# Gate/up products of an FFN as seven block products in place of eight, with the hidden tiles through DRAM

## The chip, the cores and the metric

One core of one Trainium2 chip runs the kernel. The metric is the device time in microseconds (us), a median of several executions. TensorE (PE in the profile) multiplies, VectorE (DVE) and ScalarE (ACT) work on tiles, GpSimd is POOL, and SyncE (SP) issues nearly all DMAs.

## The reference

Two blocks follow each other: a two-layer mixer (not touched here), then a hybrid layer of three attention-like mixers whose end is a gated FFN. Tokens T = 1024, model width D = 1024, hidden width 2816. All in fp32:

```python
x = layer_norm(ALPHA * x + mix @ w_out, ln1_g, ln1_b)
gu = jnp.einsum('bsd,df->bsf', x, w_gu)
gate, up = gu[..., :FFN_HIDDEN], gu[..., FFN_HIDDEN:]
ffn = jnp.einsum('bsf,fd->bsd', jax.nn.silu(gate) * up, w_down)
return layer_norm(DEEPNORM_ALPHA * x + ffn, ln2_g, ln2_b)
```

## The kernel before

Activations lie transposed: width on the 128 partitions (KT = 8 tiles k of width), tokens along the row, in two halves of 512. An fp32 product is made as three fp32r products: each operand is split in a high part (rounded) and a low part (what is left), and `w_hi*x_hi + w_lo*x_hi + w_hi*x_lo` are summed in PSUM. x1, the FFN's input, is split in `act_hi` and `act_lo`.

Weights come in **units**. SP loads a block of 128 columns (8 x 128 rows) into `w_raw[u % 2]` once the unit two before has been split. ACT rounds it into `w_hi[u % 2]` as soon as PE is done with the unit two before (`hi_at` L779, in loops `hi_next` L786), DVE makes `w_lo` (L1341, L1347), and PE multiplies. `product` (L2157) takes a unit over both halves of the tokens: 8 k x 3 x 2 = 48 matmuls of 128x512, each weight block for two of them in turn. `half_product` (L2176) takes a unit over one half, 24 matmuls; `half_pair` (L2192) does two units with their k interleaved.

The hidden width has FB = 22 tiles f of 128 columns, in GROUPS of 4, 6, 6, 6. A tile needs a gate unit and an up unit. f = 0 and 1 (SPLIT) are done by halves, while the layer norm of the second half of x1 is still under way (`x1_lo` L1858, `ln_center` L1834). For each other f, PE runs two `product`s into PSUM pairs 0 and 1, ACT takes silu of the gate (L1162), DVE multiplies by the up tile into `f_buf` (L1915), ACT rounds into `f_hi` (L1166) and DVE makes `f_lo` (L1919). After each group but the last come 8 down units, one for each output tile d (`down_rows`, L2622, PSUM pairs 2 and 3), and DVE adds each into the accumulator `z` (L1937). `z` starts as ALPHA * (x1 + bias), made by `x1_start` (L1864) in half tiles between the layer norm's steps. The last group's down products run by half for the first 512 tokens (L2192, L2176, unit U_LAST on) with transposes of z between them (L2664), and then the other way round, tokens on the partitions, for the rest (L2694), followed by the output's layer norm. In the FFN's start, PE's variance sums of the second half (L2576) wait for four `x1_start`s; the late squares are added at L1899.

PE's order of work in the FFN:

```python
for g, n in enumerate(GROUPS):
    with loop(pe, n - first) as j:
        for r, pair_used in ((0, g_act), (1, f_mul)):
            product(ug + 2 * (j + first) + r, (ug + r) % 2, r)
    if g < len(GROUPS) - 1:
        with loop(pe, KT // 2) as j:
            ...
```

Of the kernel before, what the change touches and what calls it, by code (L numbers as in the profile page):

```python
# [10 lines left out]
ALU = mybir.AluOpType  # L11
# [49 lines left out]

FG = 6
# [82 lines left out]

class Tally:
# [34 lines left out]
def build(nc, x, c, w_ada, b_ada, g_pre, w_in, w_conv, w_pool, pool_scale, w_out, g_post,  # L181
# [8 lines left out]
    x_mid = nc.dram_tensor("x_mid", [P, KT, T], FP32).ap()  # L190
    w_ada_v = w_ada.rearrange("l (p t) n -> l p t n", t=KT)

    with ExitStack() as ctx:
# [95 lines left out]
        with over() as t:  # L289
            t("under_tail", [P, 3 * KT + 1, T])  # L290
            tail = t("tail", [P, 3, T])
        arena = sb("arena", [P, ARENA])
# [16 lines left out]
        sub_gain = sb("sub_gain", [P, 1])  # L309
        index_w = sb("index_w", [P, TT, IH])  # L310
# [87 lines left out]
        U_GROUP = [U_FFN + sum(2 * n + KT for n in GROUPS[:g]) + (SPLIT if g else 0) for g in range(len(GROUPS))]  # L398
        U_LAST = U_GROUP[-1] + 2 * GROUPS[-1]
        U_END = U_LAST + 2 * KT  # L400
# [24 lines left out]

        bits_done, cand_ready, signs_done = sem("bits_done"), sem("cand_ready"), sem("signs_done")
# [46 lines left out]
        def out_stat(t, c_):  # L473

            return o_ss[:, t, c_:c_ + 1]

# [20 lines left out]
        def _(sp):  # L497
# [88 lines left out]
            def load_down(u, slot, g, d):  # L586
                n = GROUPS[g]
                sp.wait_ge(hi_ready, 1 + u)
                sp.wait_ge(lo_ready, 1 + u)
                sp.dma_start(w_raw[slot][:, 0:n, :], w_down_v[:, F_AT[g]:F_AT[g] + n, bass.ds(d * P, P)])\  # L590
                  .then_inc(raw_loaded[slot], 16)

            for g, n in enumerate(GROUPS):
                ug = U_GROUP[g]
                first = 0
                if g == 0:
                    for q in range(2 * SPLIT):
                        load(ug + q, (ug + q) % 2, w_gu(q % SPLIT // 2, q % 2))
                    ug, first = ug + SPLIT, SPLIT // 2
                with loop(sp, n - first) as j:  # L600
                    for r in range(2):
                        load(ug + 2 * (j + first) + r, (ug + r) % 2, w_gu(F_AT[g] + j + first, r))
                if g < len(GROUPS) - 1:
                    with loop(sp, KT // 2) as j:
                        for r in range(2):
                            load_down(ug + 2 * n + 2 * j + r, (ug + r) % 2, g, 2 * j + r)
            for q in range(KT):
                load_down(U_LAST + q, (U_LAST + q) % 2, len(GROUPS) - 1, q)
                if q == 1:
                    sp.dma_start(g_row[:], ln2_g.broadcast_to([P, D])).then_inc(rows_loaded, 16)  # L610
# [133 lines left out]
        def _(act):  # L744
# [419 lines left out]
            def f_rounded(f, at):  # L1164
                act.wait_ge(f_mul, 1 + f + 1)
                A(f_hi[:, bass.ds(at, 1), :], f_buf[:].rearrange("p (a t) -> p a t", a=1), ACT.Copy)\  # L1166
                    .then_inc(f_hi_done, 1)

            for f in range(SPLIT // 2):
                hi_at(U_FFN + SPLIT + 2 * f + 2)  # L1170
                gated(f, 2 * f)
                hi_at(U_FFN + SPLIT + 2 * f + 3)
                f_rounded(f, f)

            for g, n in enumerate(GROUPS):
                last = g == len(GROUPS) - 1
                ug, first = U_GROUP[g], 0
                if g == 0:
                    ug, first = ug + SPLIT, SPLIT // 2
                act.wait_ge(unit_done, 1 + ug + 2 * first + 1)  # L1180
                with loop(act, n - first) as j:
                    f = F_AT[g] + first + j
                    hi_next(ug + 2 * first, j, 2, 0)
                    gated(f, 0)
                    hi_next(ug + 2 * first, j, 2, 1)
                    f_rounded(f, first + j)
                if not last:
                    with loop(act, KT // 2) as j:
                        for r in range(2):
                            hi_next(ug + 2 * n, j, 2, r)  # L1190
# [11 lines left out]
            for d in range(KT):  # L1202
                if d + 2 < KT:
                    hi_at(U_LAST + d + 2)
# [37 lines left out]
        def _(dve):  # L1242
# [649 lines left out]

            lo_at(U_FFN + 2)
            ln_center(1, range(KT))
            x1_start(0, range(3))
# [4 lines left out]
            x1_start(0, range(3, KT))  # L1900
# [10 lines left out]
            dve.sem_inc(acc_added, 2)  # L1911

            def f_product(f, f_bank):
                dve.wait_ge(g_act, 1 + f + 1)
                v.tensor_tensor(f_buf[:], silu_buf[:], bank[f_bank + 1][:], ALU.mult).then_inc(f_mul, 1)  # L1915

            def f_low(f, at):
                dve.wait_ge(f_hi_done, f + 1)
                v.tensor_tensor(f_lo[:, bass.ds(at, 1), :].rearrange("p a t -> p (a t)"), f_buf[:],  # L1919
                                f32(f_hi[:, bass.ds(at, 1), :].rearrange("p a t -> p (a t)")), ALU.subtract)\  # L1920
                    .then_inc(f_lo_done, 1)
                dve.wait_ge(f_lo_done, f + 1)

            for f in range(SPLIT // 2):
                lo_at(U_FFN + SPLIT + 2 * f + 2)
                if f == 0:
                    x1_start(1, range(KT))
                    dve.wait_ge(acc_init, 2 * KT)
                lo_at(U_FFN + SPLIT + 2 * f + 3)
                dve.wait_ge(unit_done, 2 + U_FFN + SPLIT + 2 * f + 2)  # L1930
                f_product(f, 2 * f)
                f_low(f, f)

            def accumulate(d, b, a=None):
                zz = z[:, bass.ds(d, 1), :].rearrange("p a t -> p (a t)") if a is None else z[:, d, half(a)]
# [3 lines left out]
            for g, n in enumerate(GROUPS):  # L1939
                last = g == len(GROUPS) - 1  # L1940
                ug, first = U_GROUP[g], 0
                if g == 0:
                    ug, first = ug + SPLIT, SPLIT // 2
                dve.wait_ge(unit_done, 1 + ug + 2 * first + 1)
                with loop(dve, n - first) as j:
                    f = F_AT[g] + first + j
                    lo_next(ug + 2 * first, j, 2, 0)
                    lo_next(ug + 2 * first, j, 2, 1)
                    f_product(f, 0)
                    f_low(f, first + j)  # L1950
                if not last:
                    with loop(dve, KT // 2) as j:
                        for r in range(2):
                            dve.wait_ge(unit_done, 3 + ug + 2 * n + 2 * j + r)
                            accumulate(2 * j + r, 2 + r)
                            lo_next(ug + 2 * n, j, 2, r)
                    dve.wait_ge(acc_added, 2 + (g + 1) * KT)
# [10 lines left out]
            for d in range(KT):  # L1968
                if d + 2 < KT:
                    lo_at(U_LAST + d + 2)  # L1970
# [72 lines left out]
        def _(pe):  # L2043
# [692 lines left out]
```

## Time and profile before

| | us |
|---|---|
| median of 3 runs (lowest, highest) | 2164.23 (2163.54, 2164.96) |
| span of the profiled execution | 2160.5 |
| PE busy | 2110.7 |
| DVE busy | 1088.7 |
| ACT busy | 748.4 |
| POOL busy | 177.8 |

The span runs from the first to the last instruction of one execution; of that execution the profile gives no other time, so the runs' median stands 3.7 us above it. Engines work side by side, and their busy times overlap. DMA moved 154.75 MB, 72 GB/s in the mean.

### The profile page before, as it was taken

What the parts mean: (1) busy time and instruction counts of PE and PEld (TensorE: products, weight loads), DVE (VectorE), ACT (ScalarE), POOL (GpSimd) and SP (SyncE); (2) the same over time, 40 slices, a digit from 0 to 9 for tenths busy, and PEclk for the clock granted to TensorE, in tenths of its full rate; (3) what the DMA queues carried; (4) which work ended last, traced back from release to release, by engine and by line L of the source; (5) the groups of instructions that cost most, each with busy time, mean ns of one, the idle gap of its engine ahead of it and who ended that gap; (6) DMA issues with size and microseconds to landing.
All of it is one profiled execution on the core that took longest, in us unless ns stands there. A gap on an engine that the chain in (4) does not pass through costs nothing.

```text
span 2160.5 us, 25819 instructions
## 1 busy us (share of the span) xinstructions
PE 2110.7 (98%) x9846; PEld 1682.4 (78%) x9846; DVE 1088.7 (50%) x1701; ACT 748.4 (35%) x1191; POOL 177.8 (8%) x159
## 2 busy tenths in 40 slices
PE   8999999999999999999989998999999999999998
PEld 4888888888888877688866667778888888888877
DVE  6834463663334373888877784572422222232246
ACT  4311124431112444665766663342111111111133
POOL 1000002300000231011200000310000000000000
PEclk9999999999999999999989999999999999999999
DMA  8532333222111423101100003321211121112131
GB/s 305 166 117 88 98 106 95 76 73 69 41 47 49 134 85 88 50 22 30 49 20 1 1 21 117 90 68 53 64 49 44 44 59 49 39 49 59 46 129 78
DMA packets 222092, 154.75 MB, mean 72 GB/s; under 512 B 6565, under 2 KB 209462, under 8 KB 221878
## 3 DMA queue, kind: packets, MB, share of 16 engines
q1 hardware_dynamic: 215392, 134.53, 20.5%
q0 software_dynamic: 4608, 16.78, 2.4%
q10 hardware_dynamic: 2006, 2.31, 0.3%
q8 instruction: 53, 0.87, 0.2%
q14 instruction: 33, 0.27, 0.0%
HBM read 145.21 MB, written 8.39 MB: 71 GB/s over the span
## 4 chain that ended last, share of the span: by engine, by line
PE 84%; DVE 7%; ACT 5%; issue 2%; POOL 1%; SPq 1%; DMA 1%; DVEq 0%; ACTq 0%; POOLq 0%
PE pair L2157 37%; PE pair L2176 17%; PE pair L2622 8%; PE pair L2369 4%; PE pair L2222 3%; PE pair L2505 3%; PE pair L2473 2%; ACT proj L1007 2%; PE pair L2402 2%; PE pair L2694 2%; PE pair L2487 1%; DVE act_region L1721 1%; PE pair L2390 1%; PE pair L2192 1%; DVE w_lo L1341 1%
## 5 line engine op out<-in xcount | busy, mean ns | idle before, releaser
L1347 DVE TENSOR_TENSOR w_lo<-w_raw,w_hi 128x1024 fp32r<-128x1024 f32 x101 | 123.6, 1223 | 560.2 <-ACT w_hi L786 560.0
L786 ACT ACTIVATE w_hi<-w_raw 128x1024 fp32r<-128x1024 f32 x102 | 108.3, 1061 | 797.9 <-PE pair L2157 621.0
L2157 PE MATMUL pair<-act_hi,w_hi 128*128 128x512 f32 x1168 | 361.2, 390 | 0.0
L2157 PE MATMUL pair<-act_hi,w_lo 128*128 128x512 f32 x1168 | 359.6, 389 | 0.0
L2157 PE MATMUL pair<-act_lo,w_hi 128*128 128x512 f32 x1168 | 359.6, 389 | 0.0
L2157 PEld LDWEIGHTS pair<-act_hi,w_hi 128*128 128x128 f32 x1168 | 218.9, 188 | 46.8 <-issue 1.0
L2157 PEld LDWEIGHTS pair<-act_lo,w_hi 128*128 128x128 f32 x1168 | 219.2, 188 | 45.6
L2157 PEld LDWEIGHTS pair<-act_hi,w_lo 128*128 128x128 f32 x1168 | 219.2, 188 | 45.6
L2176 PE MATMUL pair<-act_hi,w_hi 128*128 128x512 f32 x608 | 244.4, 402 | 2.8 <-ACT act_hi L796 1.2
L2176 PE MATMUL pair<-act_lo,w_hi 128*128 128x512 f32 x608 | 238.7, 393 | 0.0
L2176 PE MATMUL pair<-act_hi,w_lo 128*128 128x512 f32 x608 | 238.2, 392 | 0.0
L1341 DVE TENSOR_TENSOR w_lo<-w_raw,w_hi 128x1024 fp32r<-128x1024 f32 x88 | 111.4, 1266 | 175.0 <-ACT w_hi L779 168.1
L779 ACT ACTIVATE w_hi<-w_raw 128x1024 fp32r<-128x1024 f32 x86 | 91.1, 1059 | 225.8 <-PE pair L2176 208.4
L2176 PEld LDWEIGHTS pair<-act_hi,w_hi 128*128 128x128 f32 x608 | 115.1, 189 | 29.9 <-issue 5.0
L2176 PEld LDWEIGHTS pair<-act_hi,w_lo 128*128 128x128 f32 x608 | 115.2, 190 | 25.6 <-issue 2.4
L2176 PEld LDWEIGHTS pair<-act_lo,w_hi 128*128 128x128 f32 x608 | 114.9, 189 | 25.1 <-DVE act_lo L1858 0.3
L2505 PEld LDWEIGHTS pair<-v_all,act_region 128*128 128x128 f32 x576 | 71.2, 196 | 32.3 <-issue 16.9
L1937 DVE TENSOR_TENSOR z<-pair,z 128x1024 f32 (+1 forms) x32 | 34.9, 1090 | 110.3 <-PE pair L2622 107.1
L2505 PE MATMUL pair<-v_all,act_region 128*128 128x128 f32 (+1 forms) x576 | 80.1, 286 | 2.0 <-ACT act_region L1071 2.0
L2622 PE MATMUL pair<-f_hi,w_hi 128*128 128x512 f32 x256 | 79.1, 390 | 0.0
L2622 PE MATMUL pair<-f_lo,w_hi 128*128 128x512 f32 x256 | 78.9, 389 | 0.0
L2622 PE MATMUL pair<-f_hi,w_lo 128*128 128x512 f32 x256 | 78.8, 389 | 0.0
(416 smaller groups left out, 3177.4 us busy)
## 6 DMA issues: line engine op xcount, KB each, us to landing
w_raw<-w_in SPq DMA_DIRECT2D x76, 512.0 KB, 3.8
w_raw<-w_out SPq DMA_DIRECT2D x48, 512.0 KB, 3.8
w_raw<-w_gu SPq DMA_DIRECT2D x48, 512.0 KB, 3.8
w_raw<-w_down SPq DMA_DIRECT2D x24, 384.0 KB, 3.2
act_region<-w_ada SPq DMA_DIRECT2D x16, 512.0 KB, 13.8
sq<-w_ada POOLq DMA_DIRECT2D x16, 512.0 KB, 4.5
sq_sum<-w_ada POOLq DMA_DIRECT2D x16, 512.0 KB, 4.9
yT<-x SPq DMA_DIRECT2D x8, 512.0 KB, 7.2
```

The source lines that it names most:

```text
L779: A(w_hi[u % 2][:], w_raw[u % 2][:], ACT.Copy).then_inc(hi_ready, 1)
L786: A(w_hi[s_][:], w_raw[s_][:], ACT.Copy).then_inc(hi_ready, 1)
L1007: A(sign_out[i], score[:, sel_at(i):sel_at(i) + keys(i)], ACT.Sign, bias=f32(cand[:, q:q + 1]), accum_out=cnt[:, q:q + 1]).then_inc(signs_ ...
L1341: v.tensor_tensor(w_lo[u % 2][:], w_raw[u % 2][:], f32(w_hi[u % 2][:]), ALU.subtract)\
L1347: v.tensor_tensor(w_lo[s_][:], w_raw[s_][:], f32(w_hi[s_][:]), ALU.subtract)\
L2157: i = mm(bank[pair][:, h * HALF:(h + 1) * HALF], w[slot][:, k, :], a[:, k, h * HALF:(h + 1) * HALF], start=(k == 0 and w is w_hi and a is ...
L2176: i_ = mm(o, w[u % 2][:, k, :], x_[:, k, tokens], start=(k == order[0] and w is w_hi and x_ is hi), stop=(k == order[-1] and x_ is lo))
L2222: i = mm(bank[pair][:, half(h)], w[slot][:, k, :], a[:, k, half(h)], start=(k == 0 and w is w_hi and a is act_hi), stop=(k == KT - 1 and w ...
L2369: i_ = mm(o, x_[:, k, t * P:(t + 1) * P], w[:, k, :], start=(k == 0 and c_ == 0), stop=(k == KT - 1 and c_ == 2))
L2402: i_ = mm(bank[pair][:, h * HALF:(h + 1) * HALF], w[u % 2][:, k, :], a[:, k, h * HALF:(h + 1) * HALF], start=(k == 0 and w is w_hi and a i ...
L2505: i_ = mm(o, probT[g % 2][:, t * P:(t + 1) * P], w, start=(t == 0), stop=(t == i))
L2622: i_ = mm(bank[2 + r][:, half(h)], w[slot][:, k, :], x_[:, k, half(h)], start=(k == 0 and w is w_hi and x_ is f_hi), stop=(k == n - 1 and ...
```

## The change

For the 20 tiles f = 2 to 21 (PAIRS), the gate and the up columns of a tile and the two halves of x1's width and of its tokens are taken as a 2x2 block product: blocks of x1 of 4 k-tiles x 512 tokens, blocks of weights of 4 k-tiles x 128 columns. The eight block products are replaced by seven (Strassen's scheme in Winograd's form): four of them need sums of x1's blocks (T1 to T4, made once by DVE and split by ACT and DVE) and four need sums of weight blocks (`weight_sums`, for each pair). A block product is `gu_product`, 12 matmuls of 128x512. Some add into a PSUM bank that holds an earlier one, others are added by DVE (`u2`, `gate1_sum`, `up_sums`), and ACT copies two out (`p1_keep`, `p5_keep`). The four halves of PSUM used by a pair alternate between pairs.

All pairs run first, then the down units of the first three groups (`down_product`), then the last group as before. The products f go from `f_buf` to DRAM (`f_mid`) and are loaded again into `f_raw` when the down units need them, to be split then. `f_raw` and `w_sum` are the same memory. All loops of the FFN are written out. `x1_start` works on whole tiles, one in each of pairs 1 to 8, in place of half tiles in the layer norm; ACT rounds and DVE splits down weights only over a group's tiles (n x 128 columns in place of 1024).

The diff, cut to its core:

```diff
+KB = KT // 2
+PAIRS = FB - SPLIT // 2
+MS = 7
...
+        M_ACT = [(x1_block(act_hi, 0, 0), x1_block(act_lo, 0, 0)), (T_HI[T4], T_LO[T4]),
+                 (x1_block(act_hi, KB, 0), x1_block(act_lo, KB, 0)), (T_HI[T1], T_LO[T1]), (T_HI[T2], T_LO[T2]),
+                 (x1_block(act_hi, KB, 1), x1_block(act_lo, KB, 1)), (T_HI[T3], T_LO[T3])]
+        M_BANK = (0, 3, 0, 1, 2, 1, 2)
+        M_MORE = (2, 5, 6)
...
+            load_pair(0)
+            keep_f(0)
+            load_pair(1)
+            keep_f(1)
+            load_pair(2)
+            for p in range(3, PAIRS):
+                keep_f(SPLIT // 2 + p - 3)
+                load_pair(p)
...
+            def m_round(p, i):
+                if p:
+                    act.wait_ge(*m_done.at(MS * (p - 1) + i + 1))
...
+                A(m_weight(True, i), m_source(i), ACT.Copy).then_inc(m_hi.sem, 1)
...
+                    down_round(0)
+                    f_round(0)
+                    f_round(1)
+                    down_round(1)
...
-            x1_start(0, range(3))
             lo_at(U_FFN + 3)
...
-            x1_start(0, range(3, KT))
+            dve.sem_inc(late_summed, 1)
             ln_root(1)
...
+                v.tensor_tensor(w_sum[:, 0], u0, u1, ALU.add).then_inc(w_summed.sem, 1)
+                dve.wait_ge(*w_summed.at(4 * p + 1))
+                v.tensor_tensor(w_sum[:, 1], w_sum[:, 0], g0, ALU.subtract).then_inc(w_summed.sem, 1)
+                dve.wait_ge(*w_summed.at(4 * p + 2))
+                v.tensor_tensor(w_sum[:, 2], g1, w_sum[:, 1], ALU.subtract).then_inc(w_summed.sem, 1)
+                v.tensor_tensor(w_sum[:, 3], g0, u0, ALU.subtract).then_inc(w_summed.sem, 1)
...
+            t_sums()
+            lo_at(U_FFN + SPLIT + 2)
+            t4_sums()
+            dve.wait_ge(unit_done, 2 + U_FFN + SPLIT + 2)
+            f_product(0, 0)
+            lo_at(U_FFN + SPLIT + 3)
+            for i, n in enumerate((T4, T1)):
+                for a in range(2):
+                    t_low(n, a)
+                m_low(0, i)
+            weight_sums(0)
...
+            for p in range(PAIRS):
+                more = p < PAIRS - 1
+                if p:
+                    m_low(p, MS - 1)
+                    up_sums(p - 1)
+                    pair_product(p - 1)
+                if p == 0:
+                    u2(p)
+                if more:
+                    weight_sums(p + 1)
+                    for i in range(4):
+                        m_low(p + 1, i)
...
+                if p:
+                    u2(p)
+                if more:
+                    m_low(p + 1, 4)
...
+                gate1_sum(p)
+                if more:
+                    m_low(p + 1, 5)
+                if 1 <= p <= KT:
+                    x1_start(p - 1)
+            up_sums(PAIRS - 1)
+            pair_product(PAIRS - 1)
...
+            for a in range(N_DOWN):
+                g, d = divmod(a, KT)
+                down_low(a + 2)
+                dve.wait_ge(unit_done, 2 + U_DOWN + a + 1)
+                if g:
+                    dve.wait_ge(acc_added, 2 + a - KT + 1)
+                accumulate(d, a % 2)
+                if d < GROUPS[g + 1]:
+                    f_low(F_AT[g + 1] + d)
...
+            def gu_product(p, i):
+
+                pe.wait_ge(*m_hi.at(MS * p + i + 1))
+                pe.wait_ge(*m_lo.at(MS * p + i + 1))
...
+                if i == 2:
+                    pe.wait_ge(*p1_kept.at(p + 1))
+                if i == 5:
+                    pe.wait_ge(*p5_kept.at(p + 1))
+                if i == 6:
+                    pe.wait_ge(*u2_made.at(p + 1))
...
+                for k in range(KB):
+                    if p == 0 and M_T[i] is not None:
+                        pe.wait_ge(*t_lo.at(2 * M_T[i] + k // 2 + 1))
+                    for w, x_ in ((hi, x_hi), (lo, x_hi), (hi, x_lo)):
+                        i_ = mm(o, w[:, k, :], x_[:, k, :], start=(k == 0 and w is hi and x_ is x_hi and i not in M_MORE),
+                                stop=(k == KB - 1 and x_ is x_lo), skip_group_check=i in M_MORE)
+                i_.then_inc(m_done.sem, 1)
...
+            for p in range(PAIRS):
+                for i in range(MS):
+                    gu_product(p, i)
+            pe.sem_inc(unit_done, 2 * PAIRS)
+            for a in range(N_DOWN):
+                down_product(a)
```

## Rows read from the trace of the kernel before

**Rows 1.** The page: span, PE's busy time, PE's granted clock in 40 slices
```profile
span 2160.5 us, 25819 instructions
...
PE 2110.7 (98%) x9846; PEld 1682.4 (78%) x9846; DVE 1088.7 (50%) x1701; ACT 748.4 (35%) x1191; POOL 177.8 (8%) x159
...
PEclk9999999999999999999989999999999999999999
```

**Rows 2.** The chain of waits over the FFN: start us, us, what
```profile
1555.27 130.74 PE pair L2157 x576
...
1686.01 65.28 PE pair L2622 x288
...
1947.13 130.57 PE pair L2157 x576
```

**Rows 3.** Windows, one gate/up stretch: us, busy by engine, PE clock, DMA share, GB/s
```profile
1555.00:1686.00 131.00, 131.00 (x579) 108.36 (x578) 27.68 (x24) 23.52 (x23) 0.00 (x0) 1.00 0.17 49
```

**Rows 4.** Timeline of the last down group's start, idle before in brackets
```profile
2077.53 0.39 PE L2192 MATMUL pair<-f_hi,w_hi 128*128 128x512 f32 x1
...
2080.20 0.19 PEld L2192 LDWEIGHTS pair<-f_hi,w_hi 128*128 128x128 f32 x1 [0.89 <-issue]
...
2083.88 0.19 PEld L2192 LDWEIGHTS pair<-f_lo,w_hi 128*128 128x128 f32 x1 [0.64 <-DVE f_lo L1919]
...
2087.46 0.19 PEld L2176 LDWEIGHTS pair<-f_hi,w_hi 128*128 128x128 f32 x1 [0.74 <-DVE z L1937]
```

**Rows 5.** Timeline of PE: first matmul of two half products, first behind them
```profile
1456.68 0.42 PE L2176 MATMUL pair<-act_hi,w_hi 128*128 128x512 f32 x1
...
1467.61 0.62 PE L2157 MATMUL pair<-act_hi,w_hi 128*128 128x512 f32 x2
```

**Rows 6.** Groups by shape, 1590 to 2160 us: busy us, mean ns | idle before
```profile
L1347 DVE TENSOR_TENSOR w_lo<-w_raw,w_hi 128x1024 fp32r<-128x1024 f32 x50 | 61.1, 1223 | 272.6 <-ACT w_hi L786 272.6
...
L786 ACT ACTIVATE w_hi<-w_raw 128x1024 fp32r<-128x1024 f32 x49 | 52.0, 1062 | 364.8 <-PE pair L2157 258.4 <-PE pair L2622 106.4
...
L1937 DVE TENSOR_TENSOR z<-pair,z 128x512 f32<-128x512 f32 x8 | 5.5, 685 | 3.2 <-PE pair L2176 3.2
```

**Rows 7.** The same view from 1380 to 1460 us, two half-tile operations
```profile
L1119 ACT ACTIVATE sq<-z 128x512 f32<-128x512 f32 x4 | 2.5, 633 | 4.8 <-DVE z L1834 3.9 <-POOL sum L734 0.9
...
L1899 DVE TENSOR_TENSOR f_buf<-f_buf,rstd_diag 128x512 f32<-128x512 f32 x1 | 0.7, 693 | 0.0
```

**Rows 8.** Timelines of DVE and PE in the FFN's start
```profile
1423.91 3.35 DVE L1864 TENSOR_SCALAR z<-z,params 128x512 f32<-128x512 f32 x3
...
1429.10 0.39 PE L2176 MATMUL pair<-act_lo,w_hi 128*128 128x512 f32 x1
...
1430.39 1.02 PE L2576 MATMUL pair<-ones,sum 128*128 128x1 f32 x8 [0.90 <-DVE z L1864]
...
1449.69 1.63 DVE L1858 SCALAR_TENSOR_TENSOR act_lo<-z,params,act_hi 128x512 fp32r<-128x512 f32 x2
...
1455.26 1.23 DVE L1341 TENSOR_TENSOR w_lo<-w_raw,w_hi 128x1024 fp32r<-128x1024 f32 x1 [3.94 <-ACT w_hi L779]
...
1456.40 3.25 DVE L1864 TENSOR_SCALAR z<-z,params 128x512 f32<-128x512 f32 x8
```

**Rows 9.** DMA issues, 1500 to 2160 us: count, KB each, us to landing
```profile
w_raw<-w_gu SPq DMA_DIRECT2D x36, 512.0 KB, 3.8
...
out<-tail SPq DMA_DIRECT2D x3, 512.0 KB, 2.6
```

**Rows 10.** Windows, columns as in rows 3, at half and at full clock
```profile
1433.40:1436.40 3.00, 3.00 (x9) 2.32 (x8) 0.28 (x1) 0.51 (x1) 0.00 (x0) 0.50 0.00 0
...
1440.30:1446.00 5.70, 3.14 (x11) 1.55 (x11) 5.28 (x8) 3.00 (x4) 0.00 (x0) 1.00 0.31 92
...
1447.00:1450.30 3.30, 3.30 (x10) 2.61 (x9) 3.30 (x6) 1.94 (x3) 0.00 (x0) 0.51 0.54 157
...
2078.00:2088.00 10.00, 8.94 (x37) 6.51 (x36) 5.41 (x5) 5.29 (x6) 0.00 (x0) 1.00 0.71 250
```

More of the change, by code:

```diff
@@ L397, in build @@
         U_FFN = U_OUT2 + 2 * KT
-        U_GROUP = [U_FFN + sum(2 * n + KT for n in GROUPS[:g]) + (SPLIT if g else 0) for g in range(len(GROUPS))]
-        U_LAST = U_GROUP[-1] + 2 * GROUPS[-1]
-        U_END = U_LAST + 2 * KT
+        U_GU = U_FFN + 2 * SPLIT
+        U_DOWN = U_GU + 2 * PAIRS
+        N_DOWN = (len(GROUPS) - 1) * KT
+        U_LAST = U_DOWN + N_DOWN
         ROW2_LN = [0, 2 * KT]
@@ L1175, in _, with t_round @@
[L1175 to L1190, printed above, removed]
+            def t_round(n, a):
+                act.wait_ge(*t_sum.at(((8, 10), (1, 2), (4, 6), (12, 14))[n][a]))
+                A(T_HI[n][:, 2 * a:2 * a + 2, :], T_RAW[n][:, 2 * a:2 * a + 2, :], ACT.Copy).then_inc(t_hi.sem, 1)
@@ new lines, in p1_keep, with p5_keep @@
+            def p1_keep(p):
+                act.wait_ge(*m_done.at(MS * p + 1))
+                if p >= 2:
+                    act.wait_ge(*up0_made.at(p - 1))
+                    act.wait_ge(*up1_made.at(p - 1))
+                A(p1_buf(p), quarter(p, 0), ACT.Copy).then_inc(p1_kept.sem, 1)
+            def p5_keep(p):
+                act.wait_ge(*m_done.at(MS * p + 4))
+                if p:
+                    act.wait_ge(*up1_made.at(p))
+                A(junk[:], quarter(p, 1), ACT.Copy).then_inc(p5_kept.sem, 1)
@@ new lines, in m_low, with u2 @@
+            def m_low(p, i):
+                dve.wait_ge(*m_hi.at(MS * p + i + 1))
+                v.tensor_tensor(m_weight(False, i), m_source(i), f32(m_weight(True, i)), ALU.subtract).then_inc(m_lo.sem, 1)
+            def u2(p):
+                dve.wait_ge(*m_done.at(MS * p + 5))
+                dve.wait_ge(*p1_kept.at(p + 1))
+                dve.wait_ge(f_mul, 1 + SPLIT // 2 + p)
+                v.tensor_tensor(silu_buf[:, half(1)], quarter(p, 2), p1_buf(p), ALU.add).then_inc(u2_made.sem, 1)
@@ new lines, in pair_product, with x1_start @@
+            def pair_product(p):
+                dve.wait_ge(*gate0_act.at(p + 1))
+                dve.wait_ge(*gate1_act.at(p + 1))
+                dve.wait_ge(*up0_made.at(p + 1))
+                dve.wait_ge(*up1_made.at(p + 1))
+                v.tensor_tensor(f_buf[:], silu_buf[:], f_buf[:], ALU.mult).then_inc(f_mul, 1)
+            def x1_start(k):
+                dve.wait_ge(*t_sum.at(14))
+                v.tensor_scalar(z[:, k, :], z[:, k, :], ln_b(k), ALPHA, ALU.add, ALU.mult).then_inc(acc_init, 1)
@@ L1934, in accumulate @@
             def accumulate(d, b, a=None):
-                zz = z[:, bass.ds(d, 1), :].rearrange("p a t -> p (a t)") if a is None else z[:, d, half(a)]
+                zz = z[:, d, :] if a is None else z[:, d, half(a)]
                 o = bank[b][:] if a is None else bank[b][:, half(a)]
                 v.tensor_tensor(zz, o, zz, ALU.add).then_inc(acc_added, 1)
[L1939 to L1957, printed above, removed]
@@ L2656, in f_split @@
+            for p in range(PAIRS):
+                for i in range(MS):
+                    gu_product(p, i)
+            pe.sem_inc(unit_done, 2 * PAIRS)
+            for a in range(N_DOWN):
+                down_product(a)
             def f_split(k, low):
```

413 lines of the change are left out of this document (321 added, 92 removed).

## The prediction

> **What bounds the kernel now.** I read the page first: TensorE (PE) is busy 98% of 2160.5 us at a granted clock of 9 tenths or more in nearly every slice [rows 1]. A busy PE may still be slow, so the second view is the chain of waits over the FFN. From 1511 to 2077 us it is nothing but matmuls: stretches of 576 of gate/up products (L2157) and of 288 of down products (L2622) in turn, each of which begins where the last ended [rows 2]. 130.74 us by 576 gives **0.227 us a matmul** of 512 columns, and 65.28 by 288 the same 0.2267: no gap at a unit's border, nor at a turn of the loops. So every matmul taken out of the FFN is worth 0.2267 us, as long as the other engines stay ahead. The third view is who does what in an FFN stretch: in 131 us with six tiles VectorE (DVE) is busy 27.7 us and ScalarE (ACT) 23.5 [rows 3]. There is much room behind PE.
>
> From 2077.7, where the third stretch of 576 ends, to 2087.5 the chain is not on PE, which looks like a stall of 9.8 us. It is not: PE ran 36 matmuls in it, worth 8.16. The timeline shows three holes: PE's weight loads waited 0.89 us (the second down weight split too late), 0.64 (last `f_lo`) and 0.74 (accumulator added late) [rows 4]. From 2077.53 to 2087.49 is 9.96 us, so 1.8 us are lost.
>
> **Matmuls removed.** Before, one hidden tile f costs 2 units x 8 k x 3 x 2 halves = 96 matmuls. After, `gu_product` makes 7 products x 4 k x 3 = 84. 20 tiles (PAIRS) take part; f = 0 and 1 stay half products. 20 x 12 = 240 matmuls x 0.2267 = **-54.4 us**. A weight now serves one matmul where in `product` it served two. The half products are already like that: 48 of them, over two units, start at 1456.68 and end their turn at 1467.61, 0.2277 each [rows 5]. Hence the weight load costs nothing visible, since one of 0.19 us [rows 4] lies beside a matmul's 0.227. The excess of 0.05 us is at the first boundary, whose weights came 0.19 us before [rows 8]; at the second one there is none. For the 140 borders between products I take 0, since the operands should be ready 2 us or more before; the other bound is 0.05 x 140 = 7 us. A gain at a border is excluded, as 0.2267 is already the pitch.
>
> **The 24 down units** of three groups keep their matmuls; they move behind the pairs: cost 0, if their operands are there (below).
>
> **DVE and ACT per pair.** A pair takes PE 84 x 0.2267 = 19.04 us (before 21.76). Half tiles of 512 cost DVE 0.68 to 0.69 from PSUM or SBUF, and whole ones 1.22; ACT 0.63 and 1.06 [rows 6, 7]. DVE does 7 `m_low`, 4 weight sums and 5 sums of products, 16 x 0.68 = 10.9, the product 1.2, and in eight pairs `x1_start`, 0.8 (before, 8 half tiles took 3.25 us [rows 8], so two take 0.8): 12.9 us. ACT: 7 roundings, 2 copies, 2 silus, 11 x 0.63 = 6.9. Both lie under 19.04. What decides is order. I put times from the start of pair p on PE, whose products end each 2.72. DVE: m_low(p,6) until 1.4, `up_sums(p-1)` and `pair_product(p-1)` until 4.8, weight sums of p+1 until 7.6, low parts 0 to 2 until 10.0. ACT waits for product 3 (10.9), copies it (11.5), rounds weight 3 (12.1); DVE low part 12.8, waits for product 4 (13.6), `u2` 14.3. PE wants `u2` for product 6 at 16.3: slack 2.0. `p1_keep` is at 3.3 for product 2 at 5.4 (slack 2.1), `p5_keep` at 11.5 for product 5 at 13.6 (2.1). Weights of p+1 are ready a product's length or more ahead, for ACT rounds each once PE has let go of its predecessor 16 us before. Behind DVE's wait for product 4 stand weight 4's low part and `gate1_sum`; their users come 13 us and 3 products later. So steady state costs **0**, with three covers of 2 us each; if one is gone, its overrun is paid in each of 19 pairs.
>
> **SP's queue and DRAM.** SP now waits for a finished product (4.8 us into the next pair) before the store, and the next weight load stands behind it. That load also waits for low part 2 at 10.0, so the store adds no wait; two loads land 3.8 us after issue [rows 9], near 18, and are wanted by ACT at 19.0 + 2.7. No store of an FFN tile is in the trace; output stores of the same 512 KB land in 2.6 us, loads in 3.8 [rows 9]. Store and reload, 22 times each, have pairs or units of time to spare, except f = 0 to 3: f_raw lies over w_sum and so they load from 1.4 us into the last pair, two by two; I get low part 3 at 16.7, before PE's 19.04. Cost 0; the bound is one load late, 3.8 us. SP's weight loads for the down units are then ahead by a unit. In a down unit (5.4 or 8.2 us) DVE does a low part, an accumulation and an f low part, at most 3.7 us, ACT 2.1: covered. f = 21 is ready 3.4 us into the down phase, and is wanted in the last group.
>
> **The start.** x1_start of the first half leaves the chain before the second half's variance. There DVE took 3.35 us for three pieces, and then those of the second call; PE had begun its half product's last matmul at 1429.10 and at a pitch of 0.227 was free at 1429.33, but its next began at 1430.39 [rows 8]. Without it PE does not wait: **-1.1 us**. After the last `x1_lo` (1451.3) DVE now has T1 and T2 first: 2 x 1.15 + 4 x 0.69 = 5.1 us, then w_lo of the next half product: 1457.6 where it was 1456.5, and PE wanted it at 1456.68 [rows 5, 8]: **+1.1 us**. Then T4 sums, product of f = 0, w_lo (1462.6), two T4 low parts, low part of weight 0 (1465.6), T1, low part 1 (1468.5), four sums (1471.2), two T2 low parts, low part 2 (1474.2); in this order `gu_product(0,0)` starts at 1468.6, product 2 could at 1474.0 and starts at 1474.2. ACT has four more of 1.06 in between and the loads of GATE and UP at 1461 and 1466; I take **+0.5** for the whole of it, bounds 0 and 3. Products 3 to 6 have T3 and `u2` ready at 1484.1 and 1484.8 for 1485.9.
>
> **The tail.** f's are ready long before; U_LAST+1's weights take 0.8 + 0.9 (768 columns) after the last down unit, under the nine matmuls (2.04 us) that `half_pair` does before it asks for them; ACT has no f to wait for. **-1.8 us**, bounds -1.8 and 0.
>
> Sum: -54.4 - 1.8 - 1.1 + 1.1 + 0.5 = **-55.7**; span 2160.5 - 55.7 = 2104.8. The runs' median is 2164.2, 3.7 above the span of the profiled execution, so **2108.5**.
>
> **The clock.** Twice in the FFN's start it is at half (1.2 GHz): 3.0 us after a 1 us pause and light matmuls of one column, 3.3 us after a stretch in which PE was idle 2.6 of 5.7 us [rows 10]. Nine and ten matmuls stood where 14 would: 1.5 us each. I leave both in place. In the tail, with three holes under 0.9 us in 10, it stayed whole [rows 10]. So small holes at borders should not lower it. The Trainium skill says otherwise in "TensorE: Matmul & The Clock Gate", section "A second HAM failure mode: psum-queue depth-cycling": a kernel that cycled through PSUM banks at each iteration paused briefly so often that its clock kept falling. The change halves the matmuls between two banks. By that rule the time would be that of rival B, 2175, and by the rows that of the sum.
>
> **Rivals.**
> A. *Borders cost.* 140 x 0.05 = 7 us: 2115.5. For: the one late border. Against: 576 matmuls without a gap. 12%.
> B. *One cover missed in each pair and the clock falls.* Place: PE at product 6 for `u2`, or 5 for `p5_keep`. A hole of 1.3 us or more, with half clock for 3 us behind it (1.5 us), makes 2.8 us a pair, and 20 x 2.8 = 56 is the point from which it decides. With a hole of 2 us: 3.5 x 19 = 66, 2108.5 + 66 = 2175, slower than before. For: a chain of six semaphores between engines per pair where there was one. Against: DVE would have to be 3.3 us later than worked out. 4%.
> C. *A cover missed by half a us*, without the clock: 19 x 0.5 = 9.5: 2118. 10%.
> D. *The low clock stretches go*, as the 1 us pause goes: -1.5 to -4.5: 2104 to 2107. For: the pause ahead of the first one goes. Against: the light matmuls and DVE's late `x1_lo` stay. 15%.
> E. *The start has a hole of 3 us more than taken*, T tiles queueing on DVE: 2111.5. 15%.
> Forecast as worked out: 44%.
>
> **Range.** A, C and E reach 2118, D 2104; unknown loads add 3.8 to one of them. 2103 to 2119 leaves out B and the far ends. Faster by over 0.2% (4.3 us, what a measurement of this kernel can tell): all but B and a larger mishap, 0.95; within 0.2% 0.01; slower 0.04.
>
> **What would show it.** PE: 1680 matmuls of `gu_product` at a pitch of 0.227 and a pair each 19.04 us; no idle of PE on `silu_buf`, `rstd_diag` or `junk`; chain all PE between the pairs and down products; DVE some 13 us of each 19. Wrong if the pitch is above 0.229 (A), if PE waits for DVE once a pair (B, C), if the clock in the pairs is under 1.00 (B), or if the handover to the down products has a hole over 1 us.

## The result and the profile after

| | before | after |
|---|---|---|
| median of 4 runs, us (lowest, highest) | 2164.24 (2163.54, 2164.96) | 2106.36 (2105.71, 2107.17) |
| ratio to before, 95% interval | | 0.9735 [0.9721, 0.9748] |
| span of the profiled execution, us | 2160.5 | 2103.6 |

The change takes 57.9 us off, 2.65%. The forecast was a median of 2108.5 and a span of 2104.8.

The page, as in [rows 1], with two rows of its DMA part:

```profile
span 2103.6 us, 25382 instructions
...
PE 2054.2 (98%) x9606; PEld 1636.5 (78%) x9606; DVE 1254.7 (60%) x1996; ACT 814.9 (39%) x1359; POOL 177.5 (8%) x159
...
PEclk9999999999999999999998999999999999999999
...
f_mid<-f_buf SPq DMA_DIRECT2D x22, 512.0 KB, 2.6
f_raw<-f_mid SPq DMA_DIRECT2D x22, 512.0 KB, 3.7
```

PE has 240 matmuls fewer (9846 to 9606) and is busy 56.5 us less, in the same share of a shorter span. DVE has 166 us more to do and ACT 66.5, and neither is seen in the time.

The chain of waits over the FFN, as in [rows 2] (L2995 is `gu_product`, L3018 `down_product`, L2542 `half_pair`, L2526 `half_product`):

```profile
1472.58 375.62 PE pair L2995 x1656
1848.20 174.08 PE pair L3018 x768
2022.28 8.36 PE pair L2542 x36
2030.64 4.33 PE pair L2526 x18
```

From 1472.58 to the tail there is nothing but matmuls, at 375.62/1656 = 0.2268 and 174.08/768 = 0.2267 us each. The handover to the down units has no hole. A stretch of this view ends with the end of its last matmul, 0.16 us after the next one has started: the timeline has the first matmul of the last group's `half_pair` at 2022.12. By the timeline this stretch takes 2030.62 - 2022.12 = 8.50 us, where it took 9.96 before [rows 4]:

```profile
2022.12 0.39 PE L2542 MATMUL pair<-f_hi,w_hi 128*128 128x512 f32 x1
...
2030.62 0.47 PE L2526 MATMUL pair<-f_hi,w_hi 128*128 128x512 f32 x1
```

All that PE itself waited for from 1380 us on (engine, line, waited for: us in total, times, longest):

```profile
PE pair L2542 <- DVE w_lo L1569: 1.8, 1, 1.8
PE pair L2526 <- DVE w_lo L1569: 0.8, 1, 0.8
PE pair L2542 <- DVE act_lo L2086: 0.7, 2, 0.4
PE pair L2526 <- DVE z L2056: 0.6, 1, 0.6
PE pair L2995 <- ACT w_hi L1321: 0.5, 1, 0.5
```

The second row and the last are the two waits that the change brings: w_lo behind T1 and T2 (L2141, L2145), and product 2 of the first pair. The view puts the last down to ACT, but product 2 also needs its own low part, which DVE finished at 1471.80 + 0.68 = 1472.48, 0.1 us before the matmul. Their places:

```profile
1455.49 0.47 PE L2526 MATMUL pair<-act_hi,w_hi 128*128 128x512 f32 x1 [0.80 <-DVE w_lo L1569]
...
1466.49 0.39 PE L2995 MATMUL pair<-act_hi,early_hi 128*128 128x512 f32 x1
...
1472.58 0.47 PE L2995 MATMUL pair<-act_hi,early_hi 128*128 128x512 f32 x1 [0.49 <-ACT w_hi L1321]
```
```profile
1471.80 0.68 DVE L2193 TENSOR_TENSOR early_lo<-w_raw,early_hi 128x512 fp32r<-128x512 f32 x1
```

DVE and ACT in the pairs, columns as in [rows 3]:

```profile
1474.00:1848.00 374.00, 374.00 (x1651) 309.68 (x1651) 241.22 (x348) 132.78 (x220) 0.00 (x0) 1.00 0.29 90
```

The 374 us hold 374/19.04 = 19.6 pairs, so DVE works 12.3 us a pair and ACT 6.8 (forecast 6.9), with the clock at 1.00. For DVE the forecast had 12.9 in the eight pairs with `x1_start` and 12.1 in the others, 12.4 in the mean. And the cover of `u2` (L2199), in one pair whose first product starts at 1638.60; product 6 starts at 1654.92, 16.3 us in:

```profile
1638.60 0.39 PE L2995 MATMUL pair<-act_hi,early_hi 128*128 128x512 f32 x1
...
1654.92 0.39 PE L2995 MATMUL pair<-act_hi,w_hi 128*128 128x512 f32 x1
```
```profile
1650.83 0.69 DVE L2193 TENSOR_TENSOR w_lo<-w_sum,w_hi 128x512 fp32r<-128x512 f32 x1 [2.03 <-ACT w_hi L1321]
1652.40 0.69 DVE L2199 TENSOR_TENSOR silu_buf<-pair,rstd_diag 128x512 f32<-128x512 f32 x1 [0.88 <-PE pair L2995]
```

`u2` ends at 1653.09, 14.5 us in; the forecast had 14.3 and a slack of 2.0, the trace 1.8. ACT's two copies in the same pair:

```profile
1641.52 0.60 ACT L1328 ACTIVATE rstd_diag<-pair 128x512 f32<-128x512 f32 x1 [2.09 <-PE pair L2995]
...
1649.68 0.60 ACT L1334 ACTIVATE junk<-pair 128x512 f32<-128x512 f32 x1 [1.60 <-PE pair L2995]
```

`p1_keep` ends at 1642.12 and product 2 starts at 1644.04, `p5_keep` ends at 1650.28 and product 5 starts at 1652.20: 1.9 us of slack each (forecast 2.1). `u2` is the tightest cover, by 0.1 us.

**Which stretches to compare.** The same first row of the FFN's start lies anywhere from 1384.88 us (e6) to 1391.70 (e10) in the traces, though nothing ahead of it was changed. So I compare two stretches of the traces. *Start*: from the variance sums of the first half (first PE row of L2576, L2926 after) to the first full gate/up matmul. *Middle*: from there to the first half product of the tail (for the kernels with all pairs ahead, where that is said, to the first down product). The rows that give the start, for before, after, e3, e4, e8 and e10 in this order, one fence a kernel:

```profile
1386.57 1.05 PE L2576 MATMUL pair<-ones,sum 128*128 128x1 f32 x8
```
```profile
1387.08 1.05 PE L2926 MATMUL pair<-ones,sum 128*128 128x1 f32 x8
```
```profile
1391.04 1.05 PE L2576 MATMUL pair<-ones,sum 128*128 128x1 f32 x8
...
1470.45 0.62 PE L2157 MATMUL pair<-act_hi,w_hi 128*128 128x512 f32 x2
```
```profile
1388.16 1.05 PE L2577 MATMUL pair<-ones,sum 128*128 128x1 f32 x8
...
1466.41 0.61 PE L2158 MATMUL pair<-act_hi,w_hi 128*128 128x512 f32 x2
```
```profile
1389.72 1.05 PE L2932 MATMUL pair<-ones,sum 128*128 128x1 f32 x8
...
1468.24 0.39 PE L3001 MATMUL pair<-act_hi,early_hi 128*128 128x512 f32 x1
```
```profile
1391.70 0.49 PE L2932 MATMUL pair<-ones,sum 128*128 128x1 f32 x3
...
1468.07 0.39 PE L3001 MATMUL pair<-act_hi,early_hi 128*128 128x512 f32 x1
```

| start, us | before | after | e3 | e4 | e8 | e10 |
|---|---|---|---|---|---|---|
| length | 81.04 | 79.41 | 79.41 | 78.25 | 78.52 | 76.37 |

Before, 1467.61 [rows 5] - 1386.57 = 81.04; after 1466.49 - 1387.08 = 79.41. The other traces of the changed kernel whose start was left as it is (e1, e2, e5, e6, e7, e9) have 79.37 to 79.42. The middle is 2087.49 - 1467.61 = 619.88 before and 2030.62 - 1466.49 = 564.13 after: -55.75. With -1.63 in the start and +0.51 ahead of it, that is the 56.9 us of the spans.

### The profile page after: what moved, and what is told of

It is laid out like the page before. It is cut to its first block, busy times and chain, and to the rows that moved or that the text cites. A ratio compares the mean times of both kernels' runs of the same rounds, so it can differ in the third digit from the quotient of the medians.

```text
span 2103.6 us, 25382 instructions
## 1 busy us (share of the span) xinstructions
PE 2054.2 (98%) x9606; PEld 1636.5 (78%) x9606; DVE 1254.7 (60%) x1996; ACT 814.9 (39%) x1359; POOL 177.5 (8%) x159
## 4 chain that ended last, share of the span: by engine, by line
PE 84%; DVE 6%; ACT 5%; issue 2%; SPq 1%; POOL 1%; DMA 1%; DVEq 0%; ACTq 0%; POOLq 0%
PE pair L2526 19%; PE pair L2995 18%; PE pair L2507 17%; PE pair L3018 8%; PE pair L2719 4%; PE pair L2572 3%; PE pair L2855 3%; PE pair L2823 2%; ACT proj L1149 2%; PE pair L2752 2%; PE pair L3066 2%; PE pair L2837 1%; DVE act_region L1949 1%; PE pair L2740 1%; PE pair L2542 1%
## 5 line engine op out<-in xcount | busy, mean ns | idle before, releaser
L2526 PE MATMUL pair<-act_hi,w_hi 128*128 128x512 f32 x608 | 243.8, 401 | 3.4 <-DVE w_lo L1569 1.6
L2526 PE MATMUL pair<-act_lo,w_hi 128*128 128x512 f32 x608 | 238.0, 391 | 0.0
L2526 PE MATMUL pair<-act_hi,w_lo 128*128 128x512 f32 x608 | 237.7, 391 | 0.0
L1569 DVE TENSOR_TENSOR w_lo<-w_raw,w_hi 128x1024 fp32r<-128x1024 f32 x80 | 102.6, 1283 | 159.2 <-ACT w_hi L921 152.2
L1575 DVE TENSOR_TENSOR w_lo<-w_raw,w_hi 128x1024 fp32r<-128x1024 f32 x37 | 45.3, 1226 | 236.7 <-ACT w_hi L928 236.5
L928 ACT ACTIVATE w_hi<-w_raw 128x1024 fp32r<-128x1024 f32 x38 | 40.3, 1061 | 345.7 <-PE pair L2507 307.0
L921 ACT ACTIVATE w_hi<-w_raw 128x1024 fp32r<-128x1024 f32 x78 | 82.6, 1059 | 211.1 <-PE pair L2526 196.0
L2507 PE MATMUL pair<-act_hi,w_hi 128*128 128x512 f32 x528 | 164.1, 392 | 0.0
L2507 PE MATMUL pair<-act_hi,w_lo 128*128 128x512 f32 x528 | 162.6, 389 | 0.0
L2507 PE MATMUL pair<-act_lo,w_hi 128*128 128x512 f32 x528 | 162.5, 389 | 0.0
L2526 PEld LDWEIGHTS pair<-act_hi,w_hi 128*128 128x128 f32 x608 | 114.8, 189 | 30.5 <-issue 5.5
L2526 PEld LDWEIGHTS pair<-act_hi,w_lo 128*128 128x128 f32 x608 | 114.8, 189 | 25.5 <-issue 2.4
L2526 PEld LDWEIGHTS pair<-act_lo,w_hi 128*128 128x128 f32 x608 | 114.6, 189 | 24.9 <-DVE act_lo L2086 0.3
L2507 PEld LDWEIGHTS pair<-act_hi,w_hi 128*128 128x128 f32 x528 | 98.9, 188 | 21.6 <-issue 0.7
L2507 PEld LDWEIGHTS pair<-act_hi,w_lo 128*128 128x128 f32 x528 | 99.1, 188 | 20.7
L2507 PEld LDWEIGHTS pair<-act_lo,w_hi 128*128 128x128 f32 x528 | 99.1, 188 | 20.7
L2193 DVE TENSOR_TENSOR w_lo<-w_sum,w_hi 128x512 fp32r<-128x512 f32 x80 | 55.1, 692 | 67.1 <-ACT w_hi L1321 67.1
L1321 ACT ACTIVATE w_hi<-w_sum 128x512 fp32r<-128x512 f32 x80 | 50.1, 629 | 92.7 <-PE pair L2995 90.9
```

The lines of the kernel that those rows point to most:

```text
L921: A(w_hi[u % 2][:], w_raw[u % 2][:], ACT.Copy).then_inc(hi_ready, 1)
L1321: A(m_weight(True, i), m_source(i), ACT.Copy).then_inc(m_hi.sem, 1)
L1569: v.tensor_tensor(w_lo[u % 2][:], w_raw[u % 2][:], f32(w_hi[u % 2][:]), ALU.subtract)\
L1575: v.tensor_tensor(w_lo[s_][:], w_raw[s_][:], f32(w_hi[s_][:]), ALU.subtract)\
L2193: v.tensor_tensor(m_weight(False, i), m_source(i), f32(m_weight(True, i)), ALU.subtract).then_inc(m_lo.sem, 1)
L2507: i = mm(bank[pair][:, h * HALF:(h + 1) * HALF], w[slot][:, k, :], a[:, k, h * HALF:(h + 1) * HALF], start=(k == 0 and w is w_hi and a is ...
```

## The experiments

Each ran beside the kernel before on the same chip (medians 2163.5, 2163.6 and 2162.5 in the three groups e1 to e4, e5 to e8, e9 and e10).

**e1. Eight products again.** In `gu_product`:

```diff
+                if i == 0:
+                    for k in range(KB):
+                        for w, x_ in ((hi, x_hi), (lo, x_hi), (hi, x_lo)):
+                            mm(o, w[:, k, :], x_[:, k, :], start=(k == 0 and w is hi and x_ is x_hi),
+                               stop=(k == KB - 1 and x_ is x_lo))
                 for k in range(KB):
```

> The changed kernel with product 0 of each pair made twice into the same PSUM bank, so eight products a pair again: 20 x 12 = 240 matmuls more, same result. My theory (the gain is the number of matmuls, at 0.2267 us each, and all else comes to -3.5 us: tail, start, clock): 2106.4 + 54.4 = 2160.8 us, no hole of PE in the pairs. Rival (part of the gain is from the new order of the work, the written-out loops or the down units in one stretch): then adding the matmuls back costs the same 54.4, but the eight-product kernel would have to stand well below the kernel before by more than the 3.5 us that the trace accounts for. Second rival (PE had free time in the pairs): less than 54.4, such as 40.

Measured: 2160.91, ratio to before 0.9985 [0.9976, 0.9995]. Two rows of its chain of waits (L2994 is the added product):

```profile
1491.75 19.04 PE pair L3000 x84
1510.79 2.72 PE pair L2994 x12
```

Each pair is 19.04 + 2.72 = 21.76 us, what two units took before. So the eighth product is the whole gain but for 2.6 us (2163.49 - 2160.91; by the interval 1.1 to 5.2). The trace accounts for 2.0 of them outside the pairs: 1.5 in the tail and 0.5 in the first group's down units (43.98 us for 192 matmuls before, which at 0.2267 are 43.5). What the new order, the loops and DRAM bring or cost besides lies within that interval.

**e2. Fewer still.** Product 3 over one k-tile:

```diff
-                for k in range(KB):
+                ks = 1 if i == 3 else KB
+                for k in range(ks):
...
-                                stop=(k == KB - 1 and x_ is x_lo), skip_group_check=i in M_MORE)
+                                stop=(k == ks - 1 and x_ is x_lo), skip_group_check=i in M_MORE)
```

> The changed kernel with product 3 of each pair over one k-tile in place of four (it leaves out three quarters of that block product): 20 x 9 = 180 matmuls fewer. My theory (PE is still the bound at seven products, with the chains of DVE and ACT 3 us ahead): -40.8 us, 2065.6, or some us more where the copy of product 3 and u2 come late, since the pair is only 17.0 us and DVE has 13 us of work in it. Rival (DVE or the chain of semaphores is the next bound close behind): less than 30 us gained and PE holes before product 5 or 6.

Measured: 2067.91, 38.5 less than the changed kernel. The gate/up stretch, from its first matmul at 1468.87 to the first down product at 1810.11 (by the chain of waits, here and below), is 341.2 us where it is 1848.20 - 1466.49 = 381.7 in the changed kernel: -40.5 of the -40.8. The 2.0 us that the runs show less lie outside it: the work ahead of the FFN ends 2.4 us later in e2's trace (variance sums at 1389.46 us, 1387.08 in the changed kernel's). PE waited 0.4 us in the stretch in all, for the copy of product 3 (`junk`), in the first pair. PE is still the only bound at 17.0 us a pair, so the covers of the other engines hold for a further tenth.

**e3. The kernel before with the FFN's loops written out.** `with loop(pe, n - first) as j:` becomes `for j in range(n - first):`, and so for the other engines and the down units.

> The kernel before with the FFN's loops written out, nothing else. My theory: 2164.2, no difference, as the trace of before shows no gap at a turn of the loops (576 matmuls in 130.57 us). Rival (written-out loops are a part of the gain): 1 to 3 us less.

Measured: 2161.87, ratio 0.9994 [0.9984, 1.0003]: no difference. The middle is 619.6 us (2090.07 - 1470.45) beside 619.9.

This run taught something by the way. Its start is 1.6 us shorter than that of the trace of before, though nothing in it was changed. The windows tell why. Both begin 0.39 us ahead of the variance sums (1430.39 before, 1434.91 in e3); first before, then e3:

```profile
1430.00:1437.00 7.00, 6.61 (x29) 5.46 (x30) 2.86 (x8) 1.15 (x2) 0.00 (x0) 0.76 0.23 66
```
```profile
1434.52:1441.52 7.00, 6.61 (x35) 5.46 (x36) 3.79 (x10) 1.30 (x3) 0.00 (x0) 1.00 0.22 63
```

The first of the two half-clock stretches of [rows 10] is not there, with the pause of 0.9 us before the variance sums in place and PE busy for the same 6.61 of 7 us, with 35 matmuls in place of 29. Nothing that e3 changes acts there, so I take it for a matter of the single execution, and e3 as the fairer measure for the start; one trace of each kernel doesn't prove it.

**e4. The kernel before, x1_start late.**

```diff
-            x1_start(0, range(3))
             lo_at(U_FFN + 3)
...
-            x1_start(0, range(3, KT))
+            dve.sem_inc(late_summed, 1)
...
                 f_product(f, 2 * f)
                 f_low(f, f)
+            x1_start(0, range(KT))
+            dve.wait_ge(acc_init, 2 * KT)
```

> The kernel before with x1_start of the first half moved behind the products of f = 0 and 1, the part of the change that concerns the layer norm alone. My theory: PE's pause of 1.06 us ahead of the variance sums of the second half goes, and with it the half-clock stretch of 3.0 us behind it (as the changed kernel's trace has it): -1.1 to -2.6 us in the start of the FFN. The first gate/up product of f = 2 starts at 1465.0 to 1466.5 where it was 1467.61. Rival (the half clock comes from the one-column matmuls of the variance): it stays, and only 1.1 us are gained.

Measured: 2161.33, ratio 0.9992 [0.9982, 1.0002], too little for the runs. Start 78.25, beside e3's 79.41: **-1.16**, the forecast's term of -1.1 and no more. In the changed kernel the start is 79.41 again. So the +1.1 for T1 and T2 ahead of w_lo is there too, and the two cancel. Theory and rival of e4 disagree on the half-clock stretch behind the variance sums. It is in neither e4's trace nor e3's, so this run doesn't decide between them.

**e5, e9, e6. How thick the cover of `u2` is.** Four, six and eight additions on DVE ahead of it:

```diff
             def u2(p):
-                dve.wait_ge(*m_done.at(MS * p + 5))
                 dve.wait_ge(*p1_kept.at(p + 1))
                 dve.wait_ge(f_mul, 1 + SPLIT // 2 + p)
+                if p:
+                    for _ in range(4):
+                        own.did(v.tensor_tensor(silu_buf[:, half(1)], p1_buf(p), p1_buf(p), ALU.add))
+                dve.wait_ge(*m_done.at(MS * p + 5))
```

> The changed kernel with four more additions of a half tile on DVE (2.9 us with their waits) ahead of u2 in each pair from the second on. The trace of the changed kernel has u2 done 13.1 us into a pair and PE wants it at 16.3: a slack of 3.2 us. My theory: u2 is done at about 15.1, PE sees nothing: 2106.4, 0 us. Rival (the slack read from the trace is not there, DVE's later work pushes back on PE): +1 us a pair or more, 20 us.

> The same with eight additions (5.8 us): u2 done about 18.0 us into the pair, 1.7 us after PE wants it. My theory: a hole of 1.7 us before product 6 in each of 19 pairs, +32 us, 2139, clock whole. Rival B of the prediction (the hole lowers the clock): another 1.5 us or more a pair, +60 us, 2167, slower than before the change. Third: the lateness adds up from pair to pair as DVE runs out of time, more than 32 us with the clock whole.

> The changed kernel with six additions ahead of u2. By e6's rows low part 3 is done 12.9 us into a pair; six additions (4.3 us) and u2 (0.7) end at 17.9, and PE wants u2 at 16.3: a hole of about 1.7 us a pair. Theory 1 (a hole costs its length and the clock stays whole, as with e5's holes of 0.4): 18 x 1.7 = 31 us, 2137. Theory 2 (a hole of this size lowers the clock for some 9 matmuls too, as e6's of 3.2 us did): 18 x 3.5 = 63 us, 2169, slower than before the change.

| | additions | median, us | from first block product to first down product | more than after | a pair (18) |
|---|---|---|---|---|---|
| after | 0 | 2106.36 | 381.7 | | |
| e5 | 4 | 2111.07 | 387.5 | 5.8 | 0.3 |
| e9 | 6 | 2140.59 | 414.6 | 32.9 | 1.8 |
| e6 | 8 | 2192.84 | 468.9 | 87.2 | 4.8 |

It is 18 pairs, for the first has no additions and in the last DVE has no low parts for a next pair to make. What PE waited for at product 6, e9 and then e6:

```profile
PE pair L2998 <- DVE silu_buf L2202: 27.8, 18, 1.5
```
```profile
PE pair L2998 <- DVE silu_buf L2202: 54.0, 18, 3.0
```

The slack of 3.2 us in the expectations of e5 and e6 was misread: I had taken the pair's start one half product too late. The rows above give 1.8, and the point from which DVE's work shows is its low part 3, done 12.9 us into the pair: 12.9 + 2.9 + 0.7 = 16.5 against 16.3, a lateness of 0.2 for e5. So e5's verdict, nothing lost, was wrong, and e5 and e9 fit once the start is right. e9's rows at product 6:

```profile
1754.97 0.39 PE L2998 MATMUL pair<-act_lo,w_hi 128*128 128x512 f32 x1
...
1756.90 0.47 PE L2998 MATMUL pair<-act_hi,w_hi 128*128 128x512 f32 x1 [1.55 <-DVE silu_buf L2202]
1757.21 0.40 PE L2998 MATMUL pair<-act_hi,w_lo 128*128 128x512 f32 x1
```

The matmuls start 1.93 us apart in place of 0.23, a hole of 1.7, and those behind it run at 0.23 again: theory 1 of e9. Over the pairs with additions the granted clock is whole, and the 32.9 us fit the 31 of theory 1:

```profile
1503.00:1883.00 380.00, 352.15 (x1533) 286.06 (x1532) 289.52 (x426) 120.15 (x200) 0.00 (x0) 1.00 0.26 80
```

e6 is another matter:

```profile
1742.19 0.51 PE L2998 MATMUL pair<-act_hi,w_hi 128*128 128x512 f32 x1 [3.00 <-DVE silu_buf L2202]
...
1742.92 0.63 PE L2998 MATMUL pair<-act_lo,w_hi 128*128 128x512 f32 x1
...
1745.06 0.63 PE L2998 MATMUL pair<-act_hi,w_lo 128*128 128x512 f32 x1
...
1745.90 0.39 PE L2998 MATMUL pair<-act_hi,w_hi 128*128 128x512 f32 x1
...
1762.68 0.39 PE L2998 MATMUL pair<-act_lo,w_hi 128*128 128x512 f32 x1
1766.07 0.50 PE L2998 MATMUL pair<-act_hi,w_hi 128*128 128x512 f32 x1 [3.00 <-DVE silu_buf L2202]
```
```profile
1742.19:1766.07 23.88, 20.88 (x84) 16.86 (x85) 16.93 (x26) 6.51 (x11) 0.00 (x0) 0.93 0.21 67
```
```profile
1503.00:1933.00 430.00, 378.90 (x1524) 305.56 (x1525) 311.16 (x457) 119.08 (x199) 0.00 (x0) 0.93 0.22 69
```

From 1762.68 to 1766.07 are 3.4 us, a hole of 3.2. Behind the hole some eight matmuls run at 0.427 us, the lower clock (1742.19 to 1745.90 is 3.71 us for nine, where 2.04 would do). The clock of the whole stretch is 0.93 as in this one pair, so it falls in all of them. 3.16 + 1.67 = 4.8 a pair, and the kernel is **slower than before the change**, 1.0139 [1.0123, 1.0154]. Rival B is a real mechanism, with its clock. The change stands 1.8 us of DVE's time a pair from where its gain begins to shrink; with e9's 4.3 us of additions it is still faster than before, with e6's 5.8 it is slower.

**e7. Each product stored twice.**

```diff
                 sp.dma_start(f_mid[:, f, :], f_buf[:]).then_inc(f_kept.sem, 16)
+                sp.dma_start(f_mid2[:, f, :], f_buf[:]).then_inc(f_kept.sem, 16)
```

and all waits on `f_kept` count 32 for 16.

> The changed kernel with each product f stored twice, to two places in DRAM, f_buf held until both have landed: 22 stores of 512 KB more. My theory: the stores are hidden, 0 us, 2106.4. Rival (the way through DRAM costs): +1 us or more, with later weight loads.

Measured: 2105.79, ratio 0.9732 [0.9717, 0.9747], beside 0.9735. The stores are free, as far as these runs can tell. Doubling the loads was not tried, for want of a place to put them.

**e8, e10. The start rearranged.** e8:

```diff
-            x1_hi(1, range(4))
+            x1_hi(1, range(2))
             hi_at(U_FFN + 5)
...
-                if k == 4:
+                if k == 3:
                     lo_at(U_FFN + 5)
...
-            t_sums()
+            t1_sums()
             lo_at(U_FFN + SPLIT + 2)
+            t2_sums()
...
+            m_low(0, 2)
             weight_sums(0)
```

and ACT rounds weight 2 of the first pair before T2. e10 has `lo_at(U_FFN + SPLIT + 3)` right behind `t2_sums` as well.

> The changed kernel with its start rearranged: the rounding and the low part of the second weight of the half pair one or two steps earlier, T1's sums before and T2's behind the low part of the next half product's weight, and low part 2 of the first pair before its weight sums. My theory: it takes away PE's holes of 1.84, 0.8 and 0.5 us and most of the half-clock stretch of some 3 us behind the first: 1.5 to 4 us less, 2103 to 2105, the pairs themselves as before. Rival (the start is bound by DVE's chain of layer norm and T sums): the holes move behind one another and nothing is gained.

> e8 with the low part of the last half product's weight ahead of T4's sums and of the product of f = 0 as well. In e8 PE waited 1.9 us for it. Theory (that wait was all that was left): the stretch from the first half's variance sums to the first block product is 76.6 us or so, where the changed kernel has 79.4 and e8 78.5; holes in the first pair none or small; the median 2 to 3 us below the changed kernel's, 2103.5 to 2105, hard to tell by the runs. Rival (DVE's backlog only moves on to the first pair): the stretch is shorter, and the first pair has holes of as much.

Measured: e8 2106.99, ratio 0.9736 [0.9723, 0.9750]; e10 2105.28, ratio 0.9730 [0.9717, 0.9744]. The runs can't tell either from the change. The traces can. In e8 the half clock is gone: the clock is 1.00 from 1440 to 1455 us, where it is 0.89 in the changed kernel. PE's wait of 1.8 us for w_lo in the half pair has become one of 1.5 for `act_lo`, and a wait of 1.9 us for the last w_lo has come:

```profile
PE pair L2548 <- DVE act_lo L2089: 2.2, 3, 1.5
PE pair L2532 <- DVE w_lo L1572: 1.9, 1, 1.9
PE pair L2532 <- DVE z L2059: 0.6, 1, 0.6
```

Start 78.52. In e10 the wait for the last w_lo goes, the one of 1.5 stays and the clock stays whole, start **76.37**; but from the first block product to the first down product it is 382.2 where e8 has 381.0 and the change 381.7: its first pair has holes. Both together, to the first down product: after 461.1, e8 459.5, e10 458.5. So e10 is 2.6 us better in its trace, of which the runs show 1.1 within their spread. Rival and theory are each half right: the half clock and the wait ahead of the last half product went, most of the hole in the half pair stayed, and part of DVE's backlog moved on.

## Why the prediction was right

- *Matmuls removed*, -54.4: shown. The price is the pitch, 0.2268 after and 0.2267 in e1, where the eighth product takes 2.72 us of each pair.
- *Borders between products*, taken as 0, other bound 7 us: 1656 matmuls take 375.62 - 0.16 = 375.46 us, 0.1 us more in all than at 0.22667 each. Rival A fell. It rested on the 0.05 us at one border whose weights came 0.19 us ahead [rows 5]; in the pairs after the first PE waited for nothing.
- *DVE and ACT per pair*, 0: shown by the one wait of 0.5 us in twenty pairs, and e2. The tightest cover was named and sized, 2.0 us against 1.8, and the two others at 2.1 against 1.9. Rival C, a cover missed by half a us, is what e5 made by hand, at 0.3 us a pair.
- *Rival B*: it did not occur, but e6 made it: its hole of 3.2 us and 1.7 us of half clock a pair. The forecast let the half clock begin with a hole of 1.3 us, and that condition is wrong: e9's hole of 1.7 left the clock whole. Its 2.8 us a pair as the break-even fits the runs: e9, at 1.8, is faster than before the change, and e6, at 4.8, slower.
- *SP's queue and DRAM*, 0: e7 for the stores; the loads land in 3.7 us, and the down units that use them run at 0.2267 us a matmul without a wait of PE.
- *Start*, -1.1 + 1.1: both shown, by e4 against e3 and by after against e4. +0.5 for the first pair: it takes 1486.28 - 1466.49 = 19.79 us, 0.75 more than 84 x 0.22667. The forecast put the wait at product 2, behind low part 2, where it is. Behind that stands the load of the first up block, which landed at 1465.58, 0.9 us ahead of the first block product. In e5 and e7 it landed 1.8 us ahead and the first pair has no hole; in e9 it was 0.9 again, and the pair loses 0.8.
- *Tail*, -1.8: 9.96 to 8.50 is -1.5. The forecast took the whole loss away, and 0.3 us of it stayed.
- *Not forecast*: the 0.5 us that the first group's down units lost before the change (see e1) are gone. They make up for what the tail gave less and the first pair cost more, so that the middle's -55.75 stands beside a forecast of -55.7 for the whole. That these errors cancel is luck.
- *The clock*: of the two half-clock stretches one is gone after. e3 lacks it too, with the pause in place, so I put the share of rival D in the result, 1.6 us of the 56.9, down to chance and not to the change. With one trace of the kernel before, that is argued and not shown.
- The rule in "TensorE: Matmul & The Clock Gate" ("A second HAM failure mode: psum-queue depth-cycling") of the Trainium skill did not apply here: 1656 matmuls in groups of 12 on changing banks ran with the clock at 1.00, and PE had no pause between the groups. The step by which the forecast applied it is wrong: before the change `product` writes its two halves of PSUM in turn, a change with each matmul (the clock was 1.00 there too [rows 3]), so the change made the switches rarer and not more frequent. e6 agrees with its second half, that repeated pauses cost a slow restart each time.

The span came 1.2 us under the forecast's, less than the 1.6 of the chance stretch, and the median lies in the range that rival D was given (2104 to 2107). The rest of the median's 2.1 is that the runs stand 2.8 us above the span of this profiled execution and not 3.7.

## What to carry to other kernels

Where a trace shows matmuls end to end at one pitch, a scheme with fewer products is worth the number removed times the pitch (e1 stands 54.5 us above the changed kernel, for 54.4), and the sums it adds are free as long as each of them meets its date. Check the dates and not the shares: DVE was busy 65% of a pair here, and 1.8 us of slack stood between it and the first wait of PE. Measure such a slack by adding work until it shows, before trusting it, and set small terms against a trace from another execution of the same kernel, since a us or two of half clock may be one execution's own.

## What the runs showed that I had not expected

A hole of 1.7 us in each 20.9 us did not lower PE's clock (e9), and one of 3.2 us in each 23.9 did in every pair, for some eight matmuls (e6), so that 1.5 us more of lateness cost 3.0 us a pair. No run has a hole between these two sizes in the pairs. The size alone does not tell: in the start of the FFN PE was idle for 0.35, 0.36 and 1.84 us within 5 us, and the clock fell behind that in every trace but those of e8 and e10, where the pauses were 0.36, 1.5 and 0.36. And two kernels that do the same up to there, with the same pause, differ in the half-clock stretch behind the variance sums: before the change it is there, in e3 it is not.
